# A two-block transformer kernel on one core: eight first slabs in buffers of their own, X's sums of squares between the modulation products, and four small edits

## What is computed

```python
def first_block(x, c, ctx, c_ctx, ...):
    for i in range(2):
        ml = silu(c) @ w_mod[i] + b_mod[i]          # 6 x 1024: shifts, scales, gates
        mc = silu(c_ctx) @ w_mod[i] + b_mod[i]
        hl = rmsnorm(xl, g_pre_mix) * (1 + ml[1]) + ml[0]
        zl = hl @ w_in[i]                            # queries, keys, conv branches
        y_l = mix_stream(zl, ...) @ w_o              # attention, conformer, short conv
        xl = xl + ml[2] * rmsnorm(y_l, g_post_mix)
        h2 = rmsnorm(xl, g_pre_mlp) * (1 + ml[4]) + ml[3]
        xl = xl + ml[5] * rmsnorm(relu(h2 @ w1) ** 2 @ w2, g_post_mlp)
        # the context stream does the same in layer 0
def second_block(x, ...):
    z = rms_norm(x) @ w_in_2                         # sparse, windowed and dilated attention
    x = x + merged @ w_o_2
    x = x + peer(rms_norm(x), ...)                   # 16384 experts, dense products with gates
```

## Time and profile before

| | |
|---|---|
| median of 3 runs | 4103.51 us (4102.27 to 4110.84) |
| the profiled execution | 4101.64 us |
| its span, first to last instruction | 4100.3 us |
| mean granted TensorE clock | 0.977 |
| PE busy | 3886.7 us (95%) |
| DVE busy | 2196.5 us (54%) |
| ACT busy | 1484.2 us (36%) |
| POOL busy | 527.8 us (13%) |

### The profile page before, as it was taken

The page is one execution under the profiler, slowest core; times in us unless marked ns, Lnnn a source line. Parts: engine busy times, 40 slices in busy tenths (PEclk is TensorE's granted clock), DMA queues, the critical chain, the costliest instruction groups (busy, mean ns, idle before and its releaser), DMA issues.

```text
span 4100.3 us, 48860 instructions
## 1 busy us (share of the span) xinstructions
PE 3886.7 (95%) x20254; PEld 3100.5 (76%) x20254; DVE 2196.5 (54%) x3857; ACT 1484.2 (36%) x1865; POOL 527.8 (13%) x748
## 2 busy tenths in 40 slices
PE   6998989999999889999899999999999999999999
PEld 4755778888875578876777878777888788888887
DVE  2275553333557464455544366888853666654444
ACT  3245532222234642234554433444444222222222
POOL 0000000000000000000002000577674111100000
PEclk8999999999999999999999999999999999999999
DMA  5410113323120023231114133445446665643332
GB/s 187 155 39 1 62 42 118 126 107 124 62 78 8 21 72 103 93 137 58 63 41 150 67 116 117 142 151 176 145 163 221 201 189 184 190 142 116 113 124 82
DMA packets 109838, 459.84 MB, mean 112 GB/s; under 512 B 9216, under 2 KB 43120, under 8 KB 68912
## 3 DMA queue, kind: packets, MB, share of 16 engines
q1 hardware_dynamic: 82048, 354.96, 24.4%
q0 software_dynamic: 27568, 101.74, 8.3%
HBM read 389.04 MB, written 67.63 MB: 111 GB/s over the span
## 4 chain that ended last, share of the span: by engine, by line
PE 83%; DVE 7%; ACT 4%; DMA 2%; POOL 1%; issue 1%; SPq 0%; DVEq 0%; ACTq 0%; POOLq 0%
PE ps L593 23%; PE ps L594 23%; PE ps L595 23%; PE ps L2616 2%; PE ps L1237 2%; DVE ACC L1438 1%; PE ps L504 1%; PE ps L672 1%; DVE MX L1411 1%; PE ps L2161 1%; POOL OH L2752 1%; PE ps L1316 1%; PE ps L2388 1%; DMA stage<-in_w_mod 1%; PE ps L2180 1%
## 5 line engine op out<-in xcount | busy, mean ns | idle before, releaser
L593 PE MATMUL ps<-HH,WH 128*128 128x512 f32 x2760 | 1058.6, 384 | 44.3 <-DVE HL L899 19.3
L594 PE MATMUL ps<-HL,WH 128*128 128x512 f32 x2760 | 1044.0, 378 | 0.0
L595 PE MATMUL ps<-HH,WL 128*128 128x512 f32 x2760 | 1040.9, 377 | 0.0
L475 DVE TENSOR_TENSOR WL<-stage,WH 128x2048 fp32r<-128x2048 f32 x246 | 563.7, 2291 | 465.4 <-ACT WH L464 465.4
L464 ACT ACTIVATE WH<-stage 128x2048 fp32r<-128x2048 f32 x246 | 469.0, 1907 | 542.8 <-PE ps L595 510.5
L593 PEld LDWEIGHTS ps<-HH,WH 128*128 128x128 f32 x2760 | 524.9, 190 | 154.9 <-issue 41.7
L595 PEld LDWEIGHTS ps<-HH,WL 128*128 128x128 f32 x2760 | 522.7, 189 | 104.3
L594 PEld LDWEIGHTS ps<-HL,WH 128*128 128x128 f32 x2760 | 524.5, 190 | 98.4 <-issue 1.2
L593 PE MATMUL ps<-AHp,WH 128*128 128x512 f32 x1024 | 403.7, 394 | 0.1
L595 PE MATMUL ps<-AHp,WL 128*128 128x512 f32 x1024 | 403.5, 394 | 0.0
L594 PE MATMUL ps<-ALp,WH 128*128 128x512 f32 x1024 | 403.5, 394 | 0.0
(11 more groups left out here) (421 smaller groups left out, 4916.0 us busy)
## 6 DMA issues: line engine op xcount, KB each, us to landing
stage<-in_w SPq DMA_DIRECT2D x64, 1024.0 KB, 4.8
stage<-in_u SPq DMA_DIRECT2D x64, 1024.0 KB, 4.8
stage<-in_v SPq DMA_DIRECT2D x64, 1024.0 KB, 4.8
stage<-in_w_mod SPq DMA_DIRECT2D x48, 1024.0 KB, 4.8
GR<-gdram POOLq DMA_DIRECT2D x32, 1024.0 KB, 8.0
AR<-adram POOLq DMA_DIRECT2D x88, 256.0 KB, 3.4
adram<-GR SPq DMA_DIRECT2D x21, 1024.0 KB, 4.5
gdram<-GST SPq DMA_DIRECT2D x16, 1024.0 KB, 5.6
```

The source lines that it names most:

```text
L475: dve.e.tensor_tensor(k.WL[o % 2][:, 0:w], k.stage[n % 2][:, 0:w], k.WH[o % 2][:, 0:w].bitcast(F32), ALU.subtract).then_inc(*dve.done("sla ...
L593: pe.e.matmul(o, wh[:, kk, cs], L.hh[:, kk, z], start=first, stop=False)
L594: pe.e.matmul(o, wh[:, kk, cs], L.hl[:, kk, z], start=False, stop=False)
L595: mm = pe.e.matmul(o, wl[:, kk, cs], L.hh[:, kk, z], start=False, stop=last)
```

## The change

1. Slabs 0 to 7 get a place each: 0 and 1 the two stage buffers, 2 to 7 six new ones over HH and HL, which are not written before the eight modulation results are there. SP sends 0 to 5 without waiting, then slab 8 (after the products of slab 0, whose place it takes), then 6 and 7, then 9 (after those of slab 1), then as before.
2. On PE and ACT, X's squares and sums come between the first four modulation slabs, two chunks ahead of each; the logarithm and exponential come after slab 3's row copy, the eight small copies after slab 4's, slab 8's split after slab 5's. DVE does slab 8's low part ahead of slab 6's steps, and layer 0's two memsets at the very start.
3. PSUM: in `tensor_linear` a group's output buffers are taken one at a time, each when its first product comes, where they were all taken ahead of the first.
4. Splits: the third slab of layer 1's `w_in` and of `win2` are split in quarters too, called after chunk 0 of the group.
5. Sums, layer ends: PE's small products come one chunk behind the down products, where they came two behind; DVE adds up chunk c right after forming it.
6. Sums, merge: the last addition on DVE goes, and PE makes two products for the sum of squares in place of one.

```diff
--- before.py
+++ after.py
...
     k.HL = h.tensor("HL", [128, 8, 768], FR)
+    k.first = k.stage + [nc.alloc_sbuf_tensor_at(f"first{n}", [128, SLAB], F32, offset=z.at + 8192 * (n - 2))
+                         for n in range(2, 8)]
...
 def landed_slab(n):
-    return f"slab{n % 2}", n
+    return f"first{n}" if n < 8 else f"slab{n % 2}", n
+
+
+def place_of(k, n):
+
+    return k.first[n] if n < 8 else k.stage[n % 2]
...
 def sync_send(k, sp, n):
...
     name, i, split, src = k.plan[n]
-    if n >= 2:
+    if n in (8, 9):
+        sp.wait_ge("mod_mm", (0, n - 8))
+    elif n >= 10:
...
             sp.wait_ge("mod_mm", k.plan[n - 2][0][1:] + (k.plan[n - 2][1],))
-    sp.e.dma_start(k.stage[n % 2][:, 0:src.shape[-1]], src).then_inc(*sp.landed(f"slab{n % 2}", n))
+    sp.e.dma_start(place_of(k, n)[:, 0:src.shape[-1]], src).then_inc(*sp.landed(*landed_slab(n)))
...
 def quarters_of(k):
...
-    return [k.slab_of[("down", l, 0), 0] for l in range(2)]
+    return [k.slab_of[name] for name in ((("down", 0, 0), 0), (("down", 1, 0), 0), (("w_in", 1), 2), ("win2", 2))]
...
 def scalar_split_quarter(k, act, n, i):
...
         p = k.psum.take(pe, ("mod", l, s))
-        w = k.stage[n % 2][:, :].rearrange("p (k n) -> p k n", k=8)
+        w = place_of(k, n)[:, :].rearrange("p (k n) -> p k n", k=8)
...
 def vector_mod(k, dve, l, s):
+    if (l, s) == (0, 6):
+        vector_split(k, dve, 8)
...
         mods = [m for s in begun for m in k.mods[L.name, s]] + (mods if not begun else [])
-        out = {c: ring.take(pe, (L.name, c), *L.ends(c)) for c in g}
+        out = {}
...
                 wh, wl = split_views(k, n, L.K)
+                if c not in out:
+                    out[c] = ring.take(pe, (L.name, c), *L.ends(c))
...
                     if n in quarters_of(k):
-                        pe.wait_ge("slab_lo", (n, kk) if kk < 3 else n)
+                        q = 4 * kk // L.K
+                        pe.wait_ge("slab_lo", (n, q) if q < 3 else n)
...
 def scalar_square_summed(k, act, name, c, src, a, b):
...
-    t = k.TA.take(act, (name, c), ("sq_sum", (name, c + 1)) if c < 7 else ("stat", (name, 7)))
+    t = k.TA.take(act, (name, c), ("sq_sum", (name, c + 1)) if c < 6 else ("stat", (name, c)))
...
 def tensor_stat_sum(k, pe, name, segs, ring=None):
     ring = ring or k.psum
-    p, t = ring.take(pe, ("stat", name), ("rstd_ln", name)), k.TA.of((name, 7))
-    pe.wait_ge("sq_sum", (name, 7))
-    for (s0, sn) in segs:
-        mm = pe.e.matmul(p[:, s0:s0 + sn], k.ones[:, :], t[:, s0:s0 + sn], start=True, stop=True)
-    mm.then_inc(*pe.done("stat", (name, 7)))
+    p = ring.take(pe, ("stat", name), ("rstd_ln", name))
+    for c in (6, 7):
+        t = k.TA.of((name, c))
+        pe.wait_ge(*(("sq_sum", (name, 6)) if c == 6 else ("square", (name, 7))))
+        for (s0, sn) in segs:
+            mm = pe.e.matmul(p[:, s0:s0 + sn], k.ones[:, :], t[:, s0:s0 + sn], start=(c == 6), stop=(c == 7))
+        mm.then_inc(*pe.done("stat", (name, c)))
...
 def tensor_stat(k, pe, name, c, n, segs, ring=None, squares=None, keep=False):
...
     dve.e.tensor_tensor(k.fold[:, :], k.ident[:, 0:64], k.ident[:, 64:128], ALU.add).then_inc(*dve.done("fold", 0))
+    for t in (k.U, k.CH):
+        op = dve.e.memset(t[:, :, :], 0.0)
+    op.then_inc(*dve.done("zeroed", (0, 1)))
...
     act.e.activation(k.csil[:, 0:16], k.cT[:, :, :].rearrange("p k v -> p (k v)"), ACT.Silu).then_inc(*act.done("csil", 0))
-    for s in range(8):
-        scalar_mod(k, act, 0, s)
...
         scalar_square(k, act, ("x", 0), c, k.X[:, c, :], 0, 768)
+        if c % 2 == 1:
+            scalar_mod(k, act, 0, c // 2)
+    scalar_rstd(k, act, ("x", 0), 8, 1024, [LAT, CTX], k.psum, norm_end(("x", 0), 8, [LAT, CTX]))
+    scalar_mod(k, act, 0, 4)
+    r, p = k.RS.take(act, "xx", ("xx_kept", 0)), k.psum.of(("stat", ("x", 0)))
+    for (s0, sn) in (LAT, CTX):
+        for q in range(4):
+            z, n = slice(32 * q, 32 * q + 32), sn // 4
+            i = act.e.activation(r[z, s0 // 4:s0 // 4 + n], p[z, s0 + n * q:s0 + n * q + n], ACT.Copy)
+    i.then_inc(*act.done("xx", 0))
+    scalar_mod(k, act, 0, 5)
+    scalar_split(k, act, 8)
+    for s in (6, 7):
+        scalar_mod(k, act, 0, s)
...
 def tensor_start(k, pe):
...
     pe.wait_ge("ones", 0)
-    for s in range(8):
-        tensor_mod(k, pe, 0, s)
...
         tensor_stat(k, pe, ("x", 0), c, 8, [LAT, CTX], keep=True)
+        if c % 2 == 1:
+            tensor_mod(k, pe, 0, c // 2)
+    for s in range(4, 8):
+        tensor_mod(k, pe, 0, s)
...
     else:
-        scalar_rstd(k, act, ("x", 0), 8, 1024, [LAT, CTX], k.psum, norm_end(("x", 0), 8, [LAT, CTX]))
-        r, p = k.RS.take(act, "xx", ("xx_kept", 0)), k.psum.of(("stat", ("x", 0)))
-        for (s0, sn) in (LAT, CTX):
-            for q in range(4):
-                z, n = slice(32 * q, 32 * q + 32), sn // 4
-                i = act.e.activation(r[z, s0 // 4:s0 // 4 + n], p[z, s0 + n * q:s0 + n * q + n], ACT.Copy)
-        i.then_inc(*act.done("xx", 0))
...
         i.then_inc(*act.done("z_act", (l, kind)))
+        if (l, c) == (1, 0):
+            for i in range(4):
+                scalar_split_quarter(k, act, k.slab_of[L.name, 2], i)
...
 def vector_z(k, dve, l):
...
         dve.wait_end("layer0", "pe", "act")
-    dve.e.memset(k.U[:, :, :], 0.0).then_inc(*dve.done("zeroed", (l, 0)))
-    dve.e.memset(k.CH[:, :, :], 0.0).then_inc(*dve.done("zeroed", (l, 1)))
+        dve.e.memset(k.U[:, :, :], 0.0).then_inc(*dve.done("zeroed", (l, 0)))
+        dve.e.memset(k.CH[:, :, :], 0.0).then_inc(*dve.done("zeroed", (l, 1)))
...
         kind, p = Z_KINDS[c], k.psum.of((L.name, c))
+        if (l, c) == (1, 0):
+            for i in range(4):
+                vector_split_quarter(k, dve, k.slab_of[L.name, 2], i)
...
                 k.psum.take(pe, ("moments", ("ymlp", l)))
-            if g == 7 and c > 1:
-                tensor_moment(k, pe, ("ymlp", l), l, c - 2, segs)
-    for c in (6, 7):
-        tensor_moment(k, pe, ("ymlp", l), l, c, segs)
+            if g == 7 and c > 0:
+                tensor_moment(k, pe, ("ymlp", l), l, c - 1, segs)
+    tensor_moment(k, pe, ("ymlp", l), l, 7, segs)
...
             if g == 7:
-                if c > 1:
-                    vector_sums(k, dve, ("ymlp", l), c - 1, a, b, False)
...
                 vector_xy(k, dve, ("ymlp", l), 3, c, segs)
+                if 0 < c < 7:
+                    vector_sums(k, dve, ("ymlp", l), c, a, b, False)
...
             act.e.activation(k.KVC[:, c, :], p[:, 0:512], ACT.Copy).then_inc(*act.done("kvc", c))
+        if c == 0:
+            for i in range(4):
+                scalar_split_quarter(k, act, k.slab_of[L.name, 2], i)
...
     for c in vector_linear(k, dve, L):
+        if c == 0:
+            for i in range(4):
+                vector_split_quarter(k, dve, k.slab_of[L.name, 2], i)
...
             vector_square_sum(k, dve, ("p", 0), c - 1, 0, 512)
-    vector_square_sum(k, dve, ("p", 0), 7, 0, 512)
...
 def sync_program(k, sp, io):
     sync_start(k, sp, io)
-    for n in range(k.slab_of[("u", 0), 0] + 3):
+    for n in (0, 1, 2, 3, 4, 5, 8, 6, 7):
+        sync_send(k, sp, n)
+    for n in range(9, k.slab_of[("u", 0), 0] + 3):
...
```

## The result

The changed kernel takes **4077.82 us** (median of 4 runs, 4077.23 to 4083.21), the kernel before in the same comparison 4104.51 (4102.27 to 4110.84, 4 runs): a ratio of 0.9934, 95% interval 0.9922 to 0.9946. That is 26.7 us faster; 4074 was forecast. The profiled execution took 4077.23 us with a span of 4075.9, against 4101.64 and 4100.3: 24.4 us, where the sum of the prediction says 29.1. The mean granted clock is 0.982 in place of 0.977.

The account below looks back on a forecast made before the run. PE, busy 95% of the span, was taken as the bound, so only its idle stretches counted. The terms sum to -29.1 us: 4101.64 gives 4072.5, as a median 4074, range 4068 to 4080, out to 4065 and 4088.

Parts of the forecast that it names:

- start: Slab loading and X's sums before the first norm: DVE starts the norm at 51.4 in place of 63.89, -12.5 us.
- PSUM, layer 0: Layer 0's first down group: three units done in the wait for the fourth buffer, 2.5 of cold clock avoided, -5.9 us.
- PSUM, layer 1: Layer 1's first down group: three units done in the wait, cold clock of 1.4 avoided, -3.8 us.
- quarters, w_in: Third slab of layer 1's w_in: PE waits for a quarter only and goes on at 1167.0, not 1169.64, -2.6 us.
- quarters, win2: Third slab of win2: the 3.10 us wait goes, with a cold restart of 1.4 to 2.5, -4.4 us.
- merge: Merge's sum: a DVE addition leaves the chain and one product joins it, -0.7 us, between 0 and -0.8.
- sums at the MLP's end: Last small products of both layers: net +0.5 in layer 0, +0.3 in layer 1, +0.8 us, between -0.3 and +1.3.
- The rival of the clock: Turns of the start: clock falls to half, a turn takes 8.4 in place of 5.0, total 4084; chance 0.14.
- The rival of a late X: Start: six slabs share the DMA engines with X, which lands up to 10 us later, total 4084; chance 0.06.
- Part 3: Rival at the first down groups: a buffer is still awaited or the cold clock stays, 4079 to 4084; chance 0.10.
- A wait in every set of small products: MLP's end: PE waits in all 14 sets, 2.7 us each, for a total slower by over 8 us; chance 0.02.
- a new wait over 1 us among the last down group's chunks: Sign at the MLP's last down group: such a wait showing there would mean the prediction is wrong.

Follow-up runs that it names:

- e4: The changed kernel with the start undone (two stage buffers, eight modulation slabs first, X's squares after them): 4092.10 us, ratio 0.9971; norm starts at 62.97.
- e2: The changed kernel with all output buffers of a group taken ahead of its first product again: 4084.18 us, ratio 0.9945.
- e3: The changed kernel with the third slabs of layer 1's w_in and of win2 split whole again: 4090.62 us, ratio 0.9964.
- e11: The changed kernel with the merge's sum as before (a last DVE addition, one product): 4079.67 us, ratio 0.9934.
- e1: The changed kernel with the edit to the sums at the MLP's end undone: 4075.16 us, ratio 0.9926.
- e8: The changed kernel with ACT's split of slab 8 in the third turn, the eight copies behind the last row, DVE's low part moved too: 4076.68 us, ratio 0.9928.

## Why the prediction was right, and where it was not

The forecast's direction, its order of the terms and most of its sizes hold. By its own steps:

| term | predicted | measured in its stretch | shown by |
|---|---|---|---|
| start | -12.5 | -12.8 | e4: +11.9 when undone |
| PSUM, layer 0 | -5.9 | -5.8 | e2: +5.6 |
| PSUM, layer 1 | -3.8 | -3.6 | e2: +3.9 |
| quarters, w_in | -2.6 | -2.7 | e3: wait of 3.12 back |
| quarters, win2 | -4.4 | -1.6 (at the slab -4.3) | e3: +3.6 (at the slab +4.6) |
| merge | -0.7 | -0.6 | e11: +0.6 |
| sums at the MLP's end | +0.8 | +1.6 and +4.3 | e1: 0.8 and 4.3 |
| rest | 0 | -3.2 | open |

- **The start** went as stepped through: turns of 5.08 us where 5.0 was said, the root at 43.2 where 42.7 was said, the low part of slab 8 done at 49.9 (49.65), the norm at 51.07 (51.4). That ACT's list and not the sums would be late is shown by e8, which moves steps of that list, with the DVE step that follows one of them, and starts 2.8 us earlier. Two slips cancelled: the kernel before had ACT's first norm step a further 0.95 us late behind the copies, which the change frees as well, and the stretch behind it became 1.0 us longer.
- **The rival of the clock** in the turns is refuted: the granted clock is 1.00 from 28 to 44 us with PE busy for 11.86 of 16. The Trainium skill ("TensorE: Matmul & The Clock Gate", "A second HAM failure mode: psum-queue depth-cycling") tells of a kernel in which small gaps between groups of products made the clock oscillate. These turns don't agree with it: their gaps of 0.87 us in 5.08 left the clock at 1.00.
- **The rival of a late X**: ACT's first square starts at 15.48 with six slabs queued behind X, where the kernel before had two. Refuted. **Part 3** does what it says: waits of 1.14 and 0.47 in place of 5.29, and the clock is kept. What it may cost in the second block stands under e2. **A wait in every set of small products**, the slower rival: the wait is there, but in four sets, not in fourteen, 4.5 us in all.
- **The step that was mis-sized** is "Net +0.5 in layer 0 and +0.3 in layer 1: +0.8, between -0.3 and +1.3". It counted the products that move and the end of the chain, and took the sets in the middle as covered, on the strength of DVE's 2.10 us of idling in a late turn. The first set has no such turn: chunks 0 and 1 end together, and in layer 1 the split of the second slab stands ahead of DVE's addition. The term is 5.9 us by the two traces and 5.1 by e1; the prediction's own sign of error, a new wait over 1 us among the last down group's chunks, is what showed.
- **win2** was sized rightly at its place, and falls short only in its stretch. From the 14th to the 111th product of the group PE takes 23.06 to 23.11 us in every kernel with quarters there, 27.41 in the kernel before and 27.62 in e3: 4.3 and 4.6 us. But the stretch gained 1.6. In it the changed kernel is 1.25 us slower at the group's start, cold for longer, 2.2 at the late wait shown under e2 and 0.7 behind that, and 1.4 faster in between. None of these places has a term in the sum.
- **Open.** The 3.2 us that the last stretch lost hold no edited line. Paired product by product they arise in small steps within the first 420 us behind the merge's norm, 1.1 us of them as waits of PE and the rest as products that are cold in the kernel before and not in the changed one. It took 1651.95 to 1654.20 us in thirteen profiles and 1655.11 in the one of the kernel before; whether that one lies apart by chance wasn't tried. With it the sum closes: 29.1 less 5.1 for the sums (5.9 - 0.8), less 2.8 for win2's stretch (4.4 - 1.6), plus 3.2, is 24.4.

## What to carry to other kernels

When work is moved one step earlier, look at the first and the last turn of its loop, not at a turn in the middle: list what each feeding engine has queued ahead of its first input. A one-off instruction there (a slab's split of 2.29 us) is the wait. Where several chains end at one point, as at this start, remove them together and then move off the path whatever is left over on the list that is last now: buffers and order brought 8.7 and 6.0 us alone, 12.8 together, and the list's tail 2.8 more. And judge an edit of a few microseconds in the stretch that it touches: the totals here hide 2 to 5 us that no edit was meant to make, most of it clock.

## What the runs showed of the hardware

- After the same wait the granted clock fell in one profile and not in the other (1.76 us of waiting at 1371.69 and 1373.23, clock 0.66 and 1.00 over the next window), with the same code up to there. Stretches with no edit take one of two times, 271.8 to 271.9 or 273.7 to 274.1 us (once 275.3) behind layer 1's norm; the one from the second block's norm takes 532.6 to 535.5 in the eleven kernels with quarters at win2 and part 3, and 529.7 in e2 without part 3.
- A long stretch in which PE hardly waits repeats to the hundredth: 433.63 us in all fourteen profiles.
- A small transfer that DVE waits for (`dv<-TD`) kept it 4.13 to 5.71 us behind ACT's last step on its source, in fourteen profiles; each time the wait of PE that hangs on it was 2.14 us or more, cold products followed, and at 1.46 and 1.47 none did.
- Six slabs queued behind X, where there were two, did not delay it: DVE's first step that needs it starts at 15.62, before at 15.66.
